# Last pair of experts: both first products ahead of both second products, last copy on two engines, samples finished second

## The reference, cut to what matters

```python
logits = xf @ w_router + b_router                 # 264 tokens, 32 experts
top_v, top_e = lax.top_k(logits, 4)
gates = softmax(top_v)
# for every block of rows that one expert got:
gu = xb @ w_e1[e] + b_e1[e]                       # w_e1[e]: 1024 x 2048
g, u = gu[:, :1024], gu[:, 1024:]
g = minimum(g, 7.0)
u = clip(u, -7.0, 7.0)
h = (u + 1.0) * (g * sigmoid(1.702 * g))
rows = h @ w_e2[e] + b_e2[e]                      # w_e2[e]: 1024 x 1024
out = segment_sum(rows * gate, token)             # added to x
y_prompt, y_sample = rms_norm(xp, g_final), rms_norm(xs, g_final)
```

## Time and profile before

| | |
|---|---|
| median of 3 runs | 1248.11 us (1247.31 to 1250.53) |
| profiled execution, its own time | 1248.22 us |
| its span | 1246.6 us |
| PE busy | 1154.3 us (93%) |
| DVE, ACT, POOL busy | 335.5, 181.5, 45.6 us |
| HBM read | 453.71 MB, 367 GB/s over the span |

### The profile page before, as it was taken

The page is one execution under the profiler, slowest core; times in us unless marked ns, Lnnn a source line. Parts: engine busy times, 40 slices in busy tenths (PEclk is TensorE's granted clock), DMA queues, the critical chain, the costliest instruction groups (busy, mean ns, idle before and its releaser), DMA issues.

```text
span 1246.6 us, 14295 instructions
## 1 busy us (share of the span) xinstructions
PE 1154.3 (93%) x5512; PEld 562.5 (45%) x5512; DVE 335.5 (27%) x814; ACT 181.5 (15%) x353; POOL 45.6 (4%) x87
## 2 busy tenths in 40 slices
PE   8999999699999999999989898989898989899896
PEld 6887888378343343334333333333232323333332
DVE  3795523615212122121212121211202021212113
ACT  3114213213010101101010101011010101010102
POOL 4000001100000000000000000000000000000000
PEclk9999999798899999999999999999999999999999
DMA  9389333894799999999999999999999999999993
GB/s 299 100 279 295 126 115 132 325 424 155 303 428 427 427 429 428 427 426 428 429 428 427 427 427 428 429 429 427 426 427 428 428 426 427 428 428 428 428 428 152
DMA packets 65576, 457.43 MB, mean 367 GB/s; under 512 B 5491, under 2 KB 34379, under 8 KB 40837
## 3 DMA queue, kind: packets, MB, share of 16 engines
q1 hardware_dynamic: 62576, 452.00, 88.3%
q10 hardware_dynamic: 1117, 3.04, 0.6%
q0 software_dynamic: 1856, 2.02, 0.6%
HBM read 453.71 MB, written 3.81 MB: 367 GB/s over the span
## 4 chain that ended last, share of the span: by engine, by line
DMA 48%; PE 45%; DVE 4%; ACT 1%; issue 1%; ACTq 0%; SPq 0%; POOL 0%; DVEq 0%
DMA ring<-in_w_e 47%; PE ps L1595 17%; PE ps L1313 11%; PE ps L1614 5%; PE ps L1332 3%; DVE ring L1004 2%; PE ps L1571 1%; PE ps L1562 1%; PE ps L1516 1%; PE ps L1475 1%; PE ps L1260 1%; PE ps L1249 1%; PE ps L1507 1%; PE ps L1604 0%; PE ps L1254 0%
## 5 line engine op out<-in xcount | busy, mean ns | idle before, releaser
L1595 PE MATMUL ps<-ring,mixed 128*64 128x512 f32 x1536 | 346.8, 596 | 39.6 <-DMA ring<-in_w_e 38.4
L1614 PE MATMUL ps<-ring,mixed 128*64 128x512 f32 x1024 | 228.3, 598 | 0.7 <-issue 0.7
L1595 PEld LDWEIGHTS ps<-ring,mixed 128*64 128x64 f32 x1536 | 105.1, 137 | 265.6 <-issue 182.0
L1154 DVE TENSOR_SCALAR mixed<-ps 128x512 f32<-128x512 f32 x32 | 22.1, 692 | 590.6 <-PE ps L1595 590.6
L1614 PEld LDWEIGHTS ps<-ring,mixed 128*64 128x64 f32 x1024 | 71.5, 137 | 155.5 <-issue 143.3
L728 ACT ACTIVATE mixed<-mixed 128x512 f32<-128x512 f32 x32 | 20.2, 630 | 521.6 <-DVE mixed L1154 521.6
L1571 PEld LDWEIGHTS ps<-mixed 128*128 128x128 f32 x512 | 64.1, 200 | 25.8 <-issue 24.3
L1571 PE MATMUL ps<-mixed 128*128 128x128 f32 x512 | 70.0, 291 | 1.3 <-ACT rstd L710 1.3
L738 ACT ACTIVATE mixed<-ps 64x512 f32<-64x512 f32 x64 | 37.8, 591 | 227.8 <-PE ps L1614 227.4
L1595 PE MATMUL ps<-mixed 128*64 128x512 f32 x256 | 58.2, 596 | 9.4 <-DMA mixed<-in_w_e 9.4
L1141 DVE SCALAR_TENSOR_TENSOR mixed<-mixed,gates 128x1024 f32<-128x1024 f32 x15 | 19.3, 1284 | 153.1 <-ACT mixed L738 153.1
(11 more groups left out here) (299 smaller groups left out, 796.1 us busy)
## 6 DMA issues: line engine op xcount, KB each, us to landing
ring<-in_w_e SPq DMA_DIRECT2D x160, 2048.0 KB, 23.3
low<-in_w_e SPq DMA_DIRECT2D x15, 2048.0 KB, 27.5
mixed<-in_w_e SPq DMA_DIRECT2D x15, 2048.0 KB, 31.9
ring<-in_w_in SPq DMA_DIRECT2D x8, 1024.0 KB, 15.6
ring<-in_cache_mem_k SPq DMA_DIRECT2D x8, 1024.0 KB, 4.8
ring<-in_cache_mem_v SPq DMA_DIRECT2D x8, 1024.0 KB, 8.5
ring<-in_w_k SPq DMA_DIRECT2D x4, 1024.0 KB, 8.9
ring<-in_w_v SPq DMA_DIRECT2D x4, 1024.0 KB, 12.6
```

Source lines behind the costliest of these rows:

```text
L1154: dve.tensor_scalar(g1, ps[0][:, :], LIMIT, None, ALU.min).then_inc(S["g_clamped"], 1)
L1595: m = pe.matmul(ps[gu][CAP * i:CAP * i + CAP, :], xeT[:, k, CAP * e2:CAP * e2 + CAP], w[:, D * gu + 512 * i:D * gu + 512 * i + 512], start ...
L1614: m = pe.matmul(ps[3][CAP * i:CAP * i + CAP, :], hTv[:, k % 4, CAP * (k // 4):CAP * (k // 4) + CAP], ring[:, s, D * (k % 2) + 512 * i:D * ...
```

## The change

SP asks for the last pieces in the order 30/4, 30/6, 31/0, 31/2, 31/4, 31/6, 30/8, 30/10, 31/8, 31/10. PE works the last pair as up 30, rounds of pair 14, turn_h 30, bias 31, up 31, transposed gates, early samples 1, down 30, turn_h 31, down 31; down 31 writes bank 0 instead of bank 3. The waits that count `freed` follow. The copy of the last result is split: ACT takes the first 512 columns, DVE the others. The last combination, its adds, norms and stores go in the order first tile, samples, second tile, and the second tile's banks are 1 and 2 instead of 0 and 1.

```diff
-LAST_BANKS = (6, 0, 4)
+LAST_BANKS = (6, 1, 4)
+FINISH = (0, 2, 1)
...
 # SP
-            rest(NE - 2, NE - 2)
+            fill(NE - 2, 4, used(NE - 3, 5))
+            fill(NE - 2, 6, used(NE - 3, 7))
             odd_half(PAIRS - 1)
-            rest(NE - 1, NE - 1)
+            fill(NE - 1, 4, used(NE - 2, 5))
+            fill(NE - 1, 6, used(NE - 2, 7))
+            fill(NE - 2, 8, used(NE - 3, 9))
+            fill(NE - 2, 10, used(NE - 3, 11))
+            fill(NE - 1, 8, W_SLOTS + used(NE - 2, 9))
+            fill(NE - 1, 10, W_SLOTS + used(NE - 2, 11))
...
-            for t in range(2):
-                sp.wait_ge(S["fin_ready"], t + 1)
-                sp.dma_start(outs["y_prompt"][0, t * P:(t + 1) * P, :], tok[:, t, :]).then_inc(S["y_stored"], 16)
-            sp.wait_ge(S["fin_ready"], 3)
-            sp.dma_start(outs["y_sample"].rearrange("b t d -> (b t) d"), tok[0:NB, 2, :]).then_inc(S["y_stored"], 16)
+            for step, t in enumerate(FINISH):
+                sp.wait_ge(S["fin_ready"], step + 1)
+                dst = outs["y_prompt"][0, t * P:(t + 1) * P, :] if t < 2 else outs["y_sample"].rearrange("b t d -> (b t) d")
+                sp.dma_start(dst, tok[0:TT[t][1], t, :]).then_inc(S["y_stored"], 16)
...
 # ACT
-            def keep_y(b, e2):
+            def keep_y(b, e2, later=0, bank=3, halves=(0, 1)):
 
-                act.wait_ge(S["freed"], RING * b + (freed_after(MOE0 - 1) + RING))
-                for i in range(2):
+                act.wait_ge(S["freed"], RING * b + (freed_after(MOE0 - 1) + RING + later))
+                for i in halves:
                     m = act.activation(ysb[CAP * e2:CAP * e2 + CAP, 512 * i:512 * i + 512],
-                                       ps[3][CAP * i:CAP * i + CAP, :], ACT.Copy)
+                                       ps[bank][CAP * i:CAP * i + CAP, :], ACT.Copy)
...
-            pair(PAIRS - 1, True)
+            half_swish(NE - 2)
+            keep_h(NE - 2)
+            half_swish(NE - 1)
+            keep_gates(PAIRS - 1)
+            keep_y(NE - 2, 0, later=W_SLOTS)
+            keep_h(NE - 1)
+            keep_y(NE - 1, 1, bank=0, halves=(0,))
...
 # DVE
-                swiglu(2 * q + 1)
+                swiglu(2 * q + 1, sooner=RING - W_SLOTS if last else 0)
...
             pair(PAIRS - 1, True)
+            dve.wait_ge(S["freed"], freed_after(MOE0 - 1) + RING * NE)
+            dve.tensor_copy(ysb[CAP:2 * CAP, 512:1024], ps[0][CAP:2 * CAP, :]).then_inc(S["y_ready"], 1)
             for t in range(2):
...
-            dve.wait_ge(S["smp_chain"], 3 + PAIRS)
-            for i in range(2):
-                dst = tok[0:NB, 2, 512 * i:512 * i + 512]
-                last = dve.tensor_tensor(dst, dst, ps[LAST_BANKS[2] + i][0:NB, :], ALU.add)
-            last.then_inc(S["smp_chain"], 1)
+                if t == 0:
+                    dve.wait_ge(S["smp_chain"], 3 + PAIRS)
+                    for i in range(2):
+                        dst = tok[0:NB, 2, 512 * i:512 * i + 512]
+                        last = dve.tensor_tensor(dst, dst, ps[LAST_BANKS[2] + i][0:NB, :], ALU.add)
+                    last.then_inc(S["smp_chain"], 1)
...
 # PE
                 up_bias(2 * q + 1)
+                if last:
+                    up(2 * q + 1, q, 1, gather_next)
+                    turn_gates(q)
+                    early_samples(1)
+                    pe.wait_ge(S["gt_ready"], q + 1)
+                    down(2 * q)
+                    turn_h(2 * q + 1)
+                    down(2 * q + 1, 0)
+                    return
                 down(2 * q)
                 up(2 * q + 1, q, 1, gather_next)
...
-            pe.wait_ge(S["y_ready"], NE)
-            for t in range(2):
+            pe.wait_ge(S["y_ready"], NE + 1)
+            for t in FINISH:
                 for i in range(2):
...
```

More of the change, by code:

```diff
@@ L732, in keep_h, with pair @@
                 act.activation(hT, ps[2][:, :], ACT.Copy, scale=0.5).then_inc(S["hT_ready"], 1)
-            def keep_y(b, e2):
-                act.wait_ge(S["freed"], RING * b + (freed_after(MOE0 - 1) + RING))
-                for i in range(2):
+            def keep_y(b, e2, later=0, bank=3, halves=(0, 1)):
+                act.wait_ge(S["freed"], RING * b + (freed_after(MOE0 - 1) + RING + later))
+                for i in halves:
                     m = act.activation(ysb[CAP * e2:CAP * e2 + CAP, 512 * i:512 * i + 512],
-                                       ps[3][CAP * i:CAP * i + CAP, :], ACT.Copy)
+                                       ps[bank][CAP * i:CAP * i + CAP, :], ACT.Copy)
                 m.then_inc(S["y_ready"], 1)
             keep_gathered(0)
-            def pair(q, last=False):
+            def pair(q):
                 half_swish(2 * q)
@@ L750, in pair @@
                 keep_h(2 * q + 1)
-                if not last:
-                    keep_gathered(q + 1)
+                keep_gathered(q + 1)
                 keep_y(2 * q + 1, 1)
@@ L771, in _ @@
             act.activation(unused, eps[:, 0:1], ACT.Sqrt)
-            for t, (t0, rows) in enumerate(TT):
+            for step, t in enumerate(FINISH):
+                rows = TT[t][1]
                 if t < 2:
@@ L778, in _ @@
                                accum_out=fss[0:rows, t:t + 1]).then_inc(S["fin_sq"], 1)
-                act.wait_ge(S["fin_sq"], t + 1)
+                act.wait_ge(S["fin_sq"], step + 1)
                 act.activation(frs[:, t:t + 1], fss[:, t:t + 1], ACT.Sqrt, bias=eps[:, 0:1], scale=1.0 / D).then_inc(S["fin_sd"], 1)
@@ L1150, in gated, with swiglu @@
                 last.then_inc(S["selg_ready"], 1)
-            def swiglu(b):
-                dve.wait_ge(S["freed"], RING * b + (freed_after(MOE0 - 1) + W_SLOTS))
+            def swiglu(b, sooner=0):
+                dve.wait_ge(S["freed"], RING * b + (freed_after(MOE0 - 1) + W_SLOTS - sooner))
                 dve.tensor_scalar(g1, ps[0][:, :], LIMIT, None, ALU.min).then_inc(S["g_clamped"], 1)
@@ L1226, in _ @@
             dve.wait_ge(S["gfin_loaded"], 16)
-            for t, (t0, rows) in enumerate(TT):
-                r = slice(0, rows)
-                dve.wait_ge(S["fin_sd"], t + 1)
+            for step, t in enumerate(FINISH):
+                r = slice(0, TT[t][1])
+                dve.wait_ge(S["fin_sd"], step + 1)
                 dve.reciprocal(frs[:, t:t + 1], frs[:, t:t + 1]).then_inc(S["fin_rec"], 1)
-                dve.wait_ge(S["fin_rec"], t + 2)
+                dve.wait_ge(S["fin_rec"], step + 2)
                 dve.scalar_tensor_tensor(out=tok[r, t, :], in0=tok[r, t, :], scalar=frs[r, t:t + 1], in1=gfin[r, :],
@@ L1605, in turn_h, with down @@
                 m.then_inc(S["h_turned"], 1)
-            def down(b):
+            def down(b, bank=3):
                 pe.wait_ge(S["hT_ready"], b + 1)
@@ L1613, in down @@
                     for i in range(2):
-                        m = pe.matmul(ps[3][CAP * i:CAP * i + CAP, :], hTv[:, k % 4, CAP * (k // 4):CAP * (k // 4) + CAP],
+                        m = pe.matmul(ps[bank][CAP * i:CAP * i + CAP, :], hTv[:, k % 4, CAP * (k // 4):CAP * (k // 4) + CAP],
                                       ring[:, s, D * (k % 2) + 512 * i:D * (k % 2) + 512 * i + 512],
@@ L1650, in pair @@
                 up_bias(2 * q + 1)
+                if last:
[7 more added lines that the diff above has]
+                    return
                 down(2 * q)
                 up(2 * q + 1, q, 1, gather_next)
-                if not last:
-                    gather(q + 1, (1,))
+                gather(q + 1, (1,))
                 pe.wait_ge(S["y_ready"], 2 * q + 1)
                 turn_gates(q)
-                if last:
-                    early_samples(1)
                 turn_h(2 * q + 1)
-                if not last:
-                    up_bias(2 * q + 2)
+                up_bias(2 * q + 2)
                 pe.wait_ge(S["gt_ready"], q + 1)
@@ L1675, in _ @@
             pair(PAIRS - 1, last=True)
-            pe.wait_ge(S["y_ready"], NE)
-            for t in range(2):
+            pe.wait_ge(S["y_ready"], NE + 1)
+            for t in FINISH:
                 for i in range(2):
[L1679 to L1683, removed]
+                    cols = ysb[:, 512 * i:512 * i + 512]
+                    if t < 2:
+                        pe.matmul(ps[LAST_BANKS[t] + i][:, :], gT[:, P * t:P * t + P], cols, start=True, stop=True).then_inc(
+                            S["comb_done"], 1)
+                    else:
+                        m = pe.matmul(ps[LAST_BANKS[2] + i][0:NB, :], pick_last, cols, start=False, stop=True)
+                if t == 2:
+                    m.then_inc(S["smp_chain"], 1)
             pe.wait_ge(S["nblk_ready"], 1)
@@ L1703, in _ @@
                     down(j + NE)
-                    pe.wait_ge(S["y_ready"], j + (NE + 1))
+                    pe.wait_ge(S["y_ready"], j + (NE + 2))
                     for t in range(2):
```

## The result

The changed kernel takes 1252.49 us (median of 17 runs, 1250.89 to 1255.09); the kernel before, beside it, 1248.11 (17 runs). The ratio is 1.0035 (1.0028 to 1.0041): 4.4 us slower. The profiled execution took 1253.21 us, span 1251.6.

The account below looks back on a forecast made before the run. The prediction took what stands behind the last first weights, a ladder of weight transfers and TensorE, as the bound. Its terms, 1.7 - 0.5 - 0.3 + 1.1 = +2.0 us, gave 1250.1 us, range 1246.5 to 1252.8.

Parts of the forecast that it names:

- Order of requests, and the hole: Weight queue: 31/8 waits for expert 30's moved product, is issued at 1218.0, 18 us later, after the queue runs empty.
- no hole: Rival: the weight queue's start from idle is covered, last landing stays 1226.6, time 1246.6; chance 0.12.
- 2 MB from idle: Transfer of 31/8 on idle engines: 7.25 us from issue to landing, ends 4.9 and 9.6; 31/10 lands 4.9 later.
- term of +1.7: Last product's end, behind the late last weights: 1233.8 against 1232.1 before, from -0.6 to +4.1.
- ScalarE's queue: Copy of 31's transposed activation, behind the copy of 30's result, ends at 1223.2; hidden by the landing at 1225.25.
- The copy: Last result's copy, shared by ScalarE and VectorE, ahead of the last combination: -0.5 us (-0.8 to -0.3).
- The adds: VectorE's adds after the last combination's start, in the new order: 6.5 instead of 6.82 us, -0.3 (-0.6 to 0).
- the three scalings are the same three: Tail after the adds: the scalings only change order, one behind another; no cost was put on them.
- The last store: End of the kernel: 512 KB instead of 32 KB are asked for last, +1.1 us (+0.7 to +1.4).
- The clock: Rival: TensorE's clock falls to half after idling ahead of the last product; time 1250.2 to 1252.2, taken 1251.2; chance 0.13.
- if the granted clock falls inside it: Sign set beforehand: the forecast is wrong if TensorE's granted clock falls inside the last product.
- Lagging engines: Rival: the last two weight transfers carry a 3.3 us engine lag anew, sum +5.3, time 1253.4; chance 0.12.

Follow-up runs that it names:

- e4: Changed kernel with the last expert's second weights in two separate free buffers, so their transfers wait for no product of expert 30: 1246.61 us, ratio 0.9987 to before.
- e7: Changed kernel plus 4 pairs of filling matmuls, on both halves of the array's columns, ahead of the last product: 1250.20 us, ratio 1.0021 to before.
- e2: Kernel before with only the last copy shared by ScalarE and VectorE: 1247.78 us, ratio 0.9997 to before.
- e9: The changed kernel measured again, nothing altered: 1251.94 us, ratio 1.0036 to before.
- e10: Changed kernel plus 2 pairs of filling matmuls ahead of the last product: 1250.74 us, ratio 1.0022 to before.
- e6: Changed kernel with the old order at the end (first tile, second tile, samples): 1251.58 us, ratio 1.0024 to before.
- e3: Changed kernel plus 8 single filling matmuls, all on one half of the array's columns, ahead of the last product: 1252.67 us, ratio 1.0033 to before.
- e8: e4 with the old end order, the last activation transposed midway through expert 30's product, the last 2 MB in two pieces: 1244.50 us, ratio 0.9973 to before.
- e11: e4 measured again, beside the same kernel with the old order at the end: 1247.08 us, ratio 0.9996 to before.

## Why the prediction was right or wrong

The time lies in the range (1246.5 to 1252.8), near its end. The sign of the likeliest case was right, its size was not: +2.0 was forecast and taken as "within 0.3%", +4.4 was measured, just over that bound. That it lies in the range is in part luck: the median is 0.3 us under the upper end, and 6 of the 17 runs, the profiled one among them, are over it. By its steps:

- **Order of requests, and the hole.** Right. 31/8 was asked for 1218.89 - 1188.22 = 30.7 us after 30/6's landing, forecast 30.4. e4 shows it as the cause. The case "no hole" (forecast 1246.6) is e4 (1246.61 and 1247.08).
- **2 MB from idle.** Mis-sized by a little: 7.6 to 8.2 us in six profiles (7.6 in five), taken 7.25; and 31/10 landed 4.9 to 6.0 after 31/8, where 4.9 was taken. With the later issue, e7's product ends 47.1 on the common scale, where the forecast has 1233.8 - 1187.6 = 46.2. The term of +1.7 measured +2.6.
- **ScalarE's queue.** Right in its place and its size: hidden by the landing, and 1.24 us where e4 takes the cover away.
- **The copy.** Right: -0.5 forecast; 0.77 instead of 1.27, and -0.5 in e2.
- **The adds.** -0.3 forecast; from the combination's start to the last add's end 1243.76 - 1237.32 = 6.44, forecast 6.5, before 6.82. But the step "the three scalings are the same three" overlooked the register read between adds and scalings: +0.5, which eats this gain.
- **The last store.** +1.1 forecast, +0.8 to +0.9 measured.
- **Sum without the clock.** The parts as measured are 2.6 - 0.5 - 0.4 + 0.5 + 0.9 = +3.1. e7 has +3.2 on the common scale and +2.6 by its ratio, against +2.0 forecast.
- **The clock.** This is the step that failed, as a chance: I gave it 0.13 and took 1251.2, and it happened in at least 10 of 17 runs. By the prediction's own sign ("if the granted clock falls inside it") it was wrong here. The rows that I read against it had gaps of 0.7 us, while the change makes one of 3.7 behind four transposes; the row that did resemble it, the end of the trace, spoke for a fall. The working was right as far as it goes: e9 is its mild case (1.7 lost, as the first half ends at 1231.3 instead of 1225.97 + 3.65 = 1229.6, all of it hidden by the wait for 31/10), the first profile of the changed kernel the worse one. The changed kernel's ratio is 0.0014 over e7's, 1.7 us, and so is e9's over e10's; from the intervals of the two ratios I estimate that each difference is uncertain by about 1.4 us or more. The split of the changed kernel's own 17 runs tells little: the ten with the low clock have a median 1.8 over the others, but in e7, where no run is that low, the four at 0.983 are 1.6 over the six above. The profiles show less, 0.4 us over the landing in the one and none in the other. So it is shown that the clock falls, where, and that it kept full speed in every profile with filling. That it costs all of the 1.7 is not shown, since the landing of 31/10 varies by 1.1 us as well: on the common scale 44.3, 43.8 and 43.6 in the three profiles with a fall (the changed kernel, e9, e6), 43.8, 43.4 and 43.2 in the three without (e3, e7, e10).
- **Lagging engines.** Wrong, as weighed: 7.6 us to landing leaves no room for 3.3 more, and e4 and e8 have the long tail of the share without harm. Why the landing of 31/10 varies by 1.1 us behind that of 31/8 no run here tells.

The Trainium skill's rule on gaps between bursts of matmuls ("TensorE: Matmul & The Clock Gate", the section on why this matters) was the better guide here than the rows with full clock: the trace of the changed kernel agrees with it, with 0.50 granted from 1225.5 after TensorE's last matmul had ended at 1223.0. The fixed cost that the Trainium skill gives ("DMA: Bandwidth & Descriptors", the anatomy of one DMA, for GpSimd's path) makes 6.8 us for 2 MB, an estimate from that page; the runs have 7.6 to 8.2.

## What to carry to other kernels

When work is moved ahead of the consumer of a buffer, ask which transfer waits for that buffer: the order of products was sound here, and its gain was lost because the last transfer was tied to slots that the moved product had not read yet; two free buffers turned +4.4 into a gain of 0.9 us on the common scale (the timed runs have it clear of noise in e4, not in e11). Price an idle stretch of TensorE by its length, for the clock may go with it. And of stores that go out last, put the small one last; what an engine does between two instructions can be uncovered by a mere change of order.

## What the runs showed of the hardware that I had not expected

- After a hole the queue doesn't start at its pace: in the changed kernel's profile 147 and 131 GB/s in the first two microseconds at a busy share of 0.7 to 0.8, against some 426 in the stream. The other five profiles with the hole have 98 to 262 there.
- Matmuls of 64 columns of weights that all go to one half of the array take 0.44 us a record for 512 columns in 32 bits, pairs on both halves 0.22 (e3 and e7). The two runs also differ in which columns of `acc` they read, so that the halves are the cause is not shown apart.
- VectorE's register read runs beside the last add in one order and at its end in the other; the first reciprocal then comes 0.54 us behind the adds instead of at once.
